# Storing two kinds of attention outputs with ScalarE instead of VectorE in a two-block transformer kernel

## Chip, core and metric

The kernel runs on one core of a Trainium2 chip. The time is that of one execution on the device, in microseconds. TensorE multiplies matrices from SBUF into PSUM (eight banks, `bank0` to `bank7`), VectorE and ScalarE read PSUM and work beside it, GpSimd prepares weights, and SyncE issues the DMAs that load them.

## What is computed

A sequence of 512 tokens of width 1024 goes through two blocks of two layers each. The first block (dilated attention, a gated recurrence, convolutional feed-forward layers) isn't touched. The second block has in each layer three attentions, whose outputs are gated and merged:

```python
o_a = _nsa(nsa_q, nsa_kv, nsa_gate, ...)          # compressed + selected + window attention, 8 heads of 64
o_a = o_a * jax.nn.silu(nsa_silu)
o_b = _fox(fox_qkv, fox_f, ...) * jax.nn.silu(fox_silu)     # forget-gated attention, 8 heads of 64
o_m = _memory_xattn(mem_q, mem_kv, ...) * jax.nn.silu(mem_silu)   # 256 memory keys, 4 heads of 128
u = g[:, :, 0] * (o_a @ w_branch_a[l]) + g[:, :, 1] * (o_b @ w_branch_b[l]) + g[:, :, 2] * (o_m @ w_branch_m[l])
x = x + u @ w_out[l]
```

Each attention is a masked softmax of scaled logits, times the values. Forget-gated and memory attention have the plain form: the value product divided by the sum of the exponentials.

## The kernel before, in words

**Tasks.** The attention of one layer of block two is cut into 128 tasks. A task is one head (a pair for compressed attention) and one tile of 128 queries. They come in four chunks of 32 (`n` = 0 to 3). In a chunk the tiles 0 and 3 are paired, then 1 and 2: two compressed tasks, eight selected and window tasks, four forget-gated (`fox`) and two memory (`mem`) ones. So fox and mem are the tasks 10 to 15 and 26 to 31 of each chunk, 32 and 16 a layer. A task has 128, 256, 384 or 512 keys.

**The pipeline.** Each engine runs through the same steps `now` = 0 to 139, in an order written out by hand, and waits on semaphores. In step `now`:

- TensorE (`pe_attend`): the logits of task `now` (L1920 mem, L1925 to L1927 fox, L1932 to L1934 selected and window, L1917 and L1918 compressed) into bank `now % 3`; then the value product of task `now - 4` (`pe_output`, L1959) into bank 5 or 6; then the transposition of the probabilities of task `now - 2` (L1944) into bank 3 or 4. In some steps a projection of 24 matmuls for a gate follows (L400 to L402, about 5.5 us; three in a chunk, at its steps 11, 18 and 25, in the first chunk at 1, 13 and 23).
- ScalarE (`act_attend`): copies the transposed probabilities of `now - 2` to SBUF (L1972), then makes the exponential of `now` (L1983, followed by a read of the accumulator, which holds the sum). Some steps add a tanh (L2019), copies of queries (L1443, L2009) or of gated outputs (L1997).
- VectorE (`dve_attend`): stores the output of `now - 5` (`dve_store`: L2130 selected and window, L2134 compressed, L2136 fox and mem), the row maximum of the logits of `now` (L2054), the reciprocal of the sum of `now - 1` (L2062), the scaled maximum of `now` (L2068) on which the exponential waits, and further small factors; in some steps halves of gates (L2098, L2104), the gating (L2111), low parts (L1451, L2116) and forget terms (L1815).

**What the stores hold up.** There are two output banks. The value product of a task waits until the store of the task two before has emptied its bank (`c.free[u] = c.s.stored[t.t]`, read by `pe_free`). The row maximum of a task waits for the store of the task six before, since they share a row of `at_st`. At steps 5, 7 and 9 of the next chunk TensorE turns the stored rows back (`pe_back`), and those wait for the last store of their kind. From step 128 on TensorE runs merge projections between the last value products.

Of the kernel before, what the change touches and what calls it, by code (L numbers as in the profile page):

```python
# [10 lines left out]
ACT = mybir.ActivationFunctionType  # L11
ALU = mybir.AluOpType
# [17 lines left out]
HD = 64  # L30
# [39 lines left out]
class Signals:  # L70
    def __init__(self, nc, ctx):
        self.every = []

        def new(name):
            self.every.append(Signal(ctx.enter_context(nc.semaphore(name))))
            return self.every[-1]


        self.unit_loaded = [new(f"unit_loaded_{s}") for s in range(SLOTS)]
        self.gains_loaded, self.ident_loaded = new("gains_loaded"), new("ident_loaded")  # L80
        self.x_loaded = [new(f"x_loaded_{k}") for k in range(DC // 2)]
        self.lru_loaded, self.taps_loaded = new("lru_cols_loaded"), new("taps_loaded")
        self.bias_loaded = [new(f"bias_loaded_{s}") for s in range(2)]
        self.consts_loaded = new("consts_loaded")
        self.w1_loaded, self.mem_loaded = new("cmp_w1_loaded"), new("mem_loaded")
        self.out_stored = new("out_stored")
        self.halves_moved = new("halves_moved")
        self.piece_hi, self.piece_split = new("piece_hi_by_act"), new("piece_split_by_vector")

        self.unit_hi, self.unit_split, self.post_added = new("unit_hi_done"), new("unit_split"), new("post_added")  # L90

        self.unit_multiplied = new("unit_multiplied")
        self.tokens_summed, self.factor_spread = new("tokens_summed"), new("factor_spread")
        self.logits_ready, self.turned = new("logits_ready"), new("turned")
        self.weighted, self.rows_turned = new("values_weighted"), new("rows_turned")
        self.rotated, self.compressed = new("rotated"), new("compressed")

        self.hi_done, self.squared = new("hi_done"), new("squared")
        self.wide_ready, self.bank_copied = new("factor_wide_ready"), new("bank_copied")
        self.exponentials, self.turned_out = new("exponentials_done"), new("turned_copied_out")  # L100
        self.rows_out, self.act_step = new("rows_copied_out"), new("function_applied")
        self.forget_biased = new("forget_biased")

        self.ones_set = new("ones_set")
        self.lo_done, self.factor_found = new("lo_done"), new("factor_found")
        self.evicted, self.residual_added = new("bank_evicted"), new("residual_added")
        self.squares_added, self.dve_step = new("squares_added"), new("vector_step_done")
        self.biased, self.maximum, self.normalized = new("logits_biased"), new("maximum_found"), new("rows_normalized")
        self.stored, self.roped = new("output_stored"), new("roped")
        self.prepared, self.gate_rows, self.short_turned_out = new("layer_prepared"), new("gate_rows_ready"), new("short_turned_copied_out")  # L110
        self.gated = new("output_gated")
        self.widened = new("factor_widened")
# [1734 lines left out]
CHUNK, TASKS, STAGE, LAST_NSA = 32, 128, 5, 25  # L1847
# [51 lines left out]

def pe_back(pe, c, layer, n, j, b):  # L1900

    pe.wait_ge(*c.s.stored["rows", layer, n, j])
    pe_free(pe, c, b)
    for i in range(TT):
        m = pe.matmul(c.bank[b][:, i * P:i * P + P], c.o_rows[n % 2][j][:, i, :], c.ident[:, :], is_transpose=True)
    c.s.rows_turned.on(m, ("back", layer, n, j))
    c.free[b] = c.s.gated["back", layer, n, j]
# [41 lines left out]
def pe_output(pe, c, t):  # L1949
    u = 5 + t.index % 2  # L1950
    o, pt, values = c.bank[u][:, 0:t.width], c.at_pt[t.index % 3], values_of(c, t)
    if t.index == 0:
        pe.wait_ge(*c.s.bank_copied["cmp", t.layer])
    if t.kind == "fox":
        pe.wait_ge(*c.s.rows_out[t.layer, 31 + t.n])
    pe.wait_ge(*c.s.turned_out[t.t])
    pe_free(pe, c, u)
    for s, v in enumerate(values):
        m = pe.matmul(o, pt[:, s * P:s * P + P], v, start=s == 0, stop=s == len(values) - 1)  # L1959
    c.s.weighted.on(m, t.t)  # L1960
    c.free[u] = c.s.stored[t.t]


def act_attend(act, c, layer):
    tasks = tasks_of(layer)
    for now in range(STEPS):
        if 0 <= now - 2 < TASKS:
            t = tasks[now - 2]
            act.wait_ge(*c.s.turned[t.t])
            if t.index >= 3:  # L1970
                act.wait_ge(*c.s.weighted[t.t - 3])
            c.s.turned_out.on(act.activation(c.at_pt[t.index % 3][:, 0:t.keys], c.bank[3 + t.index % 2][:, 0:t.keys], ACT.Copy), t.t)  # L1972
        if now < TASKS:
            t = tasks[now]
            st = c.at_st[t.index % 6]
            act.wait_ge(*c.s.maximum[t.t])
            if t.index >= 3:
                act.wait_ge(*c.s.turned[t.t - 3])
            if t.index < 2:
                act.wait_ge(*c.s.prepared["cmp_blank"])  # L1980
            for h in range(t.heads):
                keys = slice(NCP * h, NCP * h + NC) if t.kind == "cmp" else slice(0, t.keys)
                m = act.activation(probabilities(c, t)[:, keys], c.bank[t.index % 3][:, keys], ACT.Exp,  # L1983
                                   scale=exp_scale(c, t, h), bias=st[:, 2 + h:3 + h], accum_out=st[:, 4 + h:5 + h])
            c.s.exponentials.on(m, t.t)
        n, step = divmod(now, CHUNK)
        if n < 3 and step == LAST_NSA + 1:
            act.wait_ge(*c.s.logits_ready[tasks[now - 1].t])
            act_query_hi(act, c, layer, n + 1)
        if n < 4 and step == STAGE:  # L1990
            act_stage(act, c, layer, n, tasks)
        if n < 4 and step in SILU_ACT[n]:
            act_silu(act, c, layer, n, SILU_ACT[n][step])
        if n and step in BACK_HI:
            j = BACK_HI[step]
            act.wait_ge(*c.s.gated["back", layer, n - 1, j])
            c.s.hi_done.on(act.activation(c.o_hi[j][:, n - 1, :], c.o_all[:, n - 1 + 4 * j, :], ACT.Copy), ("back", layer, n - 1, j))  # L1997
# [39 lines left out]
def dve_attend(dve, c, layer):  # L2037
    z, step, tasks = c.layer_norm(layer), c.s.dve_step, tasks_of(layer)
# [2 lines left out]
    dve.memset(c.fq[0][HD:P, :], 0.0)  # L2041
    c.s.prepared.on(dve.memset(c.fq[1][0:HD, :], 0.0), ("fox_blank", layer))
    for now in range(STEPS):
        if 0 <= now - 5 < TASKS:
            dve_store(dve, c, tasks[now - 5])
        if now < TASKS:
            t = tasks[now]
            st = c.at_st[t.index % 6]
            dve.wait_ge(*c.s.logits_ready[t.t])
            if t.t >= 6:  # L2050
                dve.wait_ge(*c.s.stored[t.t - 6])
            bank = c.bank[t.index % 3]
            logits = bank[:, 0:2 * NCP].rearrange("p (g n) -> p g n", n=NCP)[:, :, 0:NC] if t.kind == "cmp" else bank[:, 0:t.keys]
            dmax = step.on(dve.reduce_max(st[:, 0:t.heads], logits, AX_X))  # L2054
        if 0 <= now - 1 < TASKS:
# [3 lines left out]
            if a.kind == "cmp":  # L2059
                d = step.on(dve.tensor_scalar(sa[:, 6:8], sa[:, 4:6], 0.5, None, ALU.max))  # L2060
# [19 lines left out]
        n, r = divmod(now, CHUNK)  # L2080
# [35 lines left out]
    c.s.lo_done.on(dve.tensor_tensor(c.o_lo[:, n + 4 * j, :], c.o_all[:, n + 4 * j, :], c.o_hi[j][:, n, :].bitcast(F32), ALU.subtract), ("back", layer, n, j))  # L2116


def dve_store(dve, c, t):
    st, o = c.at_st[t.index % 6], c.bank[5 + t.index % 2][:, 0:t.width]  # L2120
    kind = {"fox": 1, "mem": 2}.get(t.kind, 0)
    out = c.o_rows[t.n % 2][kind][:, t.i, t.j * HD:t.j * HD + t.width]
    factor = st[:, 8:9] if t.which is None else st[:, 10:11]
    dve.wait_ge(*c.s.weighted[t.t])
    dve.wait_ge(*c.s.dve_step["factor", t.t])
    if t.n >= 2 and t.kind in ("cmp", "fox", "mem"):
        dve.wait_ge(*c.s.rows_turned["back", t.layer, t.n - 2, kind])
    if t.kind in ("sel", "win"):
        dve.wait_ge(*c.s.stored[t.t - 2])
        m = dve.scalar_tensor_tensor(out, o, factor, out, ALU.mult, ALU.add)  # L2130
    elif t.kind == "cmp":
        def heads(ap):
            return ap.rearrange("p (g d) -> p g d", d=HD)
        m = dve.tensor_tensor(heads(out), heads(o), st[:, 10:12].unsqueeze(2).to_broadcast([P, 2, HD]), ALU.mult)  # L2134
    else:
        m = dve.tensor_scalar(out, o, factor, None, ALU.mult)  # L2136
    d = c.s.stored.on(m, t.t)
    c.s.stored.value["rows", t.layer, t.n, kind] = d[1]

# [401 lines left out]
```

## Time and profile before

| what | value |
| --- | --- |
| time, median of 3 runs | 3016.96 us (3015.71 to 3018.23) |
| the profiled execution, as timed | 3021.99 us |
| its span | 3020.5 us |
| TensorE busy | 2976.1 us (99%) |
| VectorE busy | 1497.1 us (50%) |
| ScalarE busy | 807.1 us (27%) |
| GpSimd busy | 1939.0 us (64%) |

Busy shares are means over the whole program; the two attention stages are 1818 to 2079 us and 2531 to 2792 us. Ends of matmuls are modelled in the profile, so that matmuls overlap in it and short stalls of TensorE show only in part as idle time. Where a stall matters, the start of one instruction is set against the end of the one that it waited for.

### The profile page before, as it was taken

What the parts mean: (1) busy time and instruction counts of PE and PEld (TensorE: products, weight loads), DVE (VectorE), ACT (ScalarE), POOL (GpSimd) and SP (SyncE); (2) the same over time, 40 slices, a digit from 0 to 9 for tenths busy, and PEclk for the clock granted to TensorE, in tenths of its full rate; (3) what the DMA queues carried; (4) which work ended last, traced back from release to release, by engine and by line L of the source; (5) the groups of instructions that cost most, each with busy time, mean ns of one, the idle gap of its engine ahead of it and who ended that gap; (6) DMA issues with size and microseconds to landing.
All of it is one profiled execution on the core that took longest, in us unless ns stands there. A gap on an engine that the chain in (4) does not pass through costs nothing.

```text
span 3020.5 us, 41671 instructions
## 1 busy us (share of the span) xinstructions
PE 2976.1 (99%) x15422; PEld 2495.9 (83%) x15422; DVE 1497.1 (50%) x3021; ACT 807.1 (27%) x1755; POOL 1939.0 (64%) x2192
## 2 busy tenths in 40 slices
PE   9999999999999999999999999999999999999999
PEld 7888887888888878888888887788888988888887
DVE  3333334477730684777213746663334654664332
ACT  1111111322210452222112225552112213564110
POOL 6555554599987788999775862125777684112775
PEclk9999999999999999999999999999999999999999
DMA  4222232122332222323323221011224332011232
GB/s 168 93 90 89 93 105 67 57 98 98 98 98 98 72 82 77 98 98 98 111 91 126 94 95 43 29 36 64 98 98 140 100 103 70 29 43 36 91 98 91
DMA packets 70216, 261.47 MB, mean 87 GB/s; under 512 B 8320, under 2 KB 8832, under 8 KB 68224
## 3 DMA queue, kind: packets, MB, share of 16 engines
q1 hardware_dynamic: 65696, 232.81, 23.6%
q10 hardware_dynamic: 4320, 25.99, 2.4%
q8 instruction: 125, 2.05, 0.3%
q14 instruction: 75, 0.61, 0.1%
HBM read 251.43 MB, written 2.10 MB: 84 GB/s over the span
## 4 chain that ended last, share of the span: by engine, by line
PE 88%; POOL 5%; DVE 3%; issue 2%; ACT 2%; DMA 0%; ACTq 0%; DVEq 0%; SPq 0%; POOLq 0%
PE bank L400 23%; PE bank L402 23%; PE bank L401 23%; POOL w_lo L2314 3%; PE bank L1959 3%; PE bank L1944 1%; PE bank L708 1%; POOL w_hi L2310 1%; PE bank L427 1%; PE bank L440 1%; PE bank L432 1%; PE bank L1660 1%; PE bank L428 1%; PE bank L680 1%; PE bank L1366 1%
## 5 line engine op out<-in xcount | busy, mean ns | idle before, releaser
L2314 POOL TENSOR_TENSOR w_lo<-w_raw,w_hi 128x256 fp32r<-128x256 f32 x1728 | 1406.7, 844 | 36.1
L2310 POOL TENSOR_SCALAR w_hi<-w_raw 128x1024 fp32r<-128x1024 f32 x432 | 489.9, 1134 | 1014.6 <-PE bank L402 918.7
L400 PE MATMUL bank<-in_hi,w_hi 128*128 128x512 f32 x1408 | 554.8, 394 | 0.7 <-POOL w_lo L2314 0.7
L402 PE MATMUL bank<-in_hi,w_lo 128*128 128x512 f32 x1408 | 548.6, 390 | 0.0
L401 PE MATMUL bank<-in_lo,w_hi 128*128 128x512 f32 x1408 | 547.8, 389 | 0.0
L400 PE MATMUL bank<-z_hi,w_hi 128*128 128x512 f32 x976 | 392.4, 402 | 0.4 <-POOL w_lo L2314 0.4
L402 PE MATMUL bank<-z_hi,w_lo 128*128 128x512 f32 x976 | 381.2, 391 | 0.0
L401 PE MATMUL bank<-z_lo,w_hi 128*128 128x512 f32 x976 | 380.7, 390 | 0.0
L402 PEld LDWEIGHTS bank<-in_hi,w_lo 128*128 128x128 f32 x1408 | 264.3, 188 | 56.0
L400 PEld LDWEIGHTS bank<-in_hi,w_hi 128*128 128x128 f32 x1408 | 264.5, 188 | 53.0 <-issue 1.1
L401 PEld LDWEIGHTS bank<-in_lo,w_hi 128*128 128x128 f32 x1408 | 264.7, 188 | 52.8
L400 PEld LDWEIGHTS bank<-z_hi,w_hi 128*128 128x128 f32 x976 | 183.9, 188 | 39.3 <-issue 3.7
L401 PEld LDWEIGHTS bank<-z_lo,w_hi 128*128 128x128 f32 x976 | 184.0, 189 | 38.8 <-issue 2.9
L402 PEld LDWEIGHTS bank<-z_hi,w_lo 128*128 128x128 f32 x976 | 183.5, 188 | 39.3
L2054 DVE TENSOR_REDUCE at_st<-bank 128x1 f32<-128x256 f32 (+4 forms) x256 | 113.0, 441 | 131.9 <-PE bank L1927 69.7
L400 PE MATMUL bank<-ffn_hidden_hi,w_hi 128*128 128x512 f32 x384 | 149.6, 390 | 0.0
L402 PE MATMUL bank<-ffn_hidden_hi,w_lo 128*128 128x512 f32 x384 | 149.4, 389 | 0.0
L401 PE MATMUL bank<-ffn_hidden_lo,w_hi 128*128 128x512 f32 x384 | 149.4, 389 | 0.0
L1972 ACT ACTIVATE at_pt<-bank 128x256 f32<-128x256 f32 (+3 forms) x256 | 104.2, 407 | 163.4 <-PE bank L1944 161.7
L662 DVE TENSOR_TENSOR out_squares<-out_squares,square 128x512 f32<-128x512 f32 x28 | 28.2, 1009 | 229.9 <-ACT square L653 229.7
L1018 DVE TENSOR_TENSOR ffn_raw<-bank,factor_wide 128x512 f32<-128x512 f32 x96 | 65.4, 684 | 116.4 <-PE bank L402 107.8
L772 ACT ACTIVATE logit<-logit,stat 128x768 f32<-128x768 f32 x32 | 30.0, 937 | 281.1 <-DVE stat L830 281.1
(441 smaller groups left out, 5161.5 us busy)
## 6 DMA issues: line engine op xcount, KB each, us to landing
w_raw<-in_units SPq DMA_DIRECT2D x434, 512.0 KB, 3.4
bias<-in_bias ACTq DMA_DIRECT2D x8, 1152.0 KB, 5.1
o_all<-in_cmp_w ACTq DMA_DIRECT2D x4, 2048.0 KB, 8.5
x_res<-in_x ACTq DMA_DIRECT2D x4, 512.0 KB, 7.6
mem_in<-in_mem ACTq DMA_DIRECT2D x2, 1024.0 KB, 8.6
nsa_q_hi<-nsa_q_hi SPq DMA_DIRECT2D x16, 128.0 KB, 2.5
nsa_q_lo<-nsa_q_lo SPq DMA_DIRECT2D x16, 128.0 KB, 2.3
out<-x_res ACTq DMA_DIRECT2D x4, 512.0 KB, 2.6
```

Of the source, the lines that this page charges most:

```text
L400: pe.matmul(out, hi[:, w], rh, start=start and n == 0, stop=False)
L401: pe.matmul(out, hi[:, w], rl, start=False, stop=False)
L402: last = pe.matmul(out, lo[:, w], rh, start=False, stop=stop and n == len(tiles) - 1)
L427: pe.matmul(out, c.w_hi[(first + u) % SLOTS][:, w], hi[:, k, :], start=k == 0, stop=False)
L428: pe.matmul(out, c.w_lo[(first + u) % SLOTS][:, w], hi[:, k, :], start=False, stop=False)
L432: last = pe.matmul(out, c.w_hi[(first + u) % SLOTS][:, w], lo[:, k, :], start=False, stop=k == DC - 1)
L1018: c.s.evicted.on(dve.tensor_tensor(c.raw[half][:, :], c.bank[2 * (n % 3) + half][:, :], z.wide, ALU.mult), ("up", layer, n, half))
L1959: m = pe.matmul(o, pt[:, s * P:s * P + P], v, start=s == 0, stop=s == len(values) - 1)
L1972: c.s.turned_out.on(act.activation(c.at_pt[t.index % 3][:, 0:t.keys], c.bank[3 + t.index % 2][:, 0:t.keys], ACT.Copy), t.t)
L2054: dmax = step.on(dve.reduce_max(st[:, 0:t.heads], logits, AX_X))
L2310: d = c.s.unit_hi.on(pool.tensor_scalar(c.w_hi[s][:, :], c.w_raw[s][:, :], 1.0, 0.0, ALU.mult, ALU.add))
L2314: last = pool.tensor_tensor(c.w_lo[s][:, w], c.w_raw[s][:, w], c.w_hi[s][:, w].bitcast(F32), ALU.subtract)
```

## The change

Fox and mem tasks, 48 a layer, are stored by ScalarE (`act_store`) with one copy that has a scale per partition (the reciprocal). It stands in ScalarE's step `now = t + 4`, behind the exponential, where VectorE stored in its step `t + 5`, at its start. These stores count on a semaphore of their own (`copied_out`), and TensorE's value product, `pe_back` and VectorE's row maximum wait on the one or the other after the kind of task. The new instruction waits for the value product, the factor and, from the third chunk on, for the turning of the rows that it overwrites. Stores of compressed, selected and window tasks stay with VectorE.

```diff
@@ pe_back
-    pe.wait_ge(*c.s.stored["rows", layer, n, j])
+    pe.wait_ge(*(c.s.copied_out if j else c.s.stored)["rows", layer, n, j])
@@ pe_output
-    c.free[u] = c.s.stored[t.t]
+    c.free[u] = stored(c, t)
@@ act_attend, behind the exponential
+        if 0 <= now - 4 < TASKS and by_act(tasks[now - 4]):
+            act_store(act, c, tasks[now - 4])
@@ dve_attend
-        if 0 <= now - 5 < TASKS:
+        if 0 <= now - 5 < TASKS and not by_act(tasks[now - 5]):
             dve_store(dve, c, tasks[now - 5])
...
-                dve.wait_ge(*c.s.stored[t.t - 6])
+                dve.wait_ge(*stored(c, t, 6))
@@ new
+def by_act(t):
+
+    return t.which is None
+
+
+def stored(c, t, back=0):
+    every = tasks_of(t.layer) if t.index >= back else tasks_of(t.layer - 1)
+    t = every[(t.index - back) % TASKS]
+    return (c.s.copied_out if by_act(t) else c.s.stored)[t.t]
+
+
+def act_store(act, c, t):
+    st, o = c.at_st[t.index % 6], c.bank[5 + t.index % 2][:, 0:t.width]
+    kind = {"fox": 1, "mem": 2}[t.kind]
+    act.wait_ge(*c.s.weighted[t.t])
+    act.wait_ge(*c.s.dve_step["factor", t.t])
+    if t.n >= 2:
+        act.wait_ge(*c.s.rows_turned["back", t.layer, t.n - 2, kind])
+    d = c.s.copied_out.on(act.activation(c.o_rows[t.n % 2][kind][:, t.i, t.j * HD:t.j * HD + t.width], o, ACT.Copy, scale=st[:, 8:9]), t.t)
+    c.s.copied_out.value["rows", t.layer, t.n, kind] = d[1]
@@ dve_store
-    else:
-        m = dve.tensor_scalar(out, o, factor, None, ALU.mult)
```

## Rows read from the trace of the kernel before

**Rows 1.** The page: busy us (share of the span) xinstructions of each engine.

```profile
PE 2976.1 (99%) x15422; PEld 2495.9 (83%) x15422; DVE 1497.1 (50%) x3021; ACT 807.1 (27%) x1755; POOL 1939.0 (64%) x2192
```

**Rows 2.** Windows view: length, busy us (instructions) of PE, PEld, DVE, ACT, POOL, then clock, DMA.

```profile
1880.00:1910.00 30.00, 28.12 (x198) 23.83 (x197) 20.75 (x91) 19.42 (x61) 3.82 (x5) 1.00 0.06 19
```

**Rows 3.** The chain that ended last: start us, us, what.

```profile
1904.58 0.53 ACT fox_q L2019
...
1905.73 0.29 DVE o_rows L2136
```

**Rows 4.** Waits in the first attention stage: us in total, times, longest.

```profile
PE bank L1959 <- DVE o_rows L2130: 4.0, 7, 1.0
...
PE bank L1959 <- DVE o_rows L2134: 2.4, 6, 0.5
PE bank L1959 <- DVE o_rows L2136: 1.9, 7, 0.4
```

**Rows 5.** Groups of the whole run by shape, VectorE: busy us, mean ns | idle before.

```profile
L2136 DVE TENSOR_SCALAR o_rows<-bank,at_st 128x64 f32<-128x64 f32 x64 | 17.8, 278 | 10.5 <-PE bank L1959 10.5
...
L2136 DVE TENSOR_SCALAR o_rows<-bank,at_st 128x128 f32<-128x128 f32 x32 | 11.1, 347 | 22.9 <-PE bank L1959 22.9
```

**Rows 6.** The same of ScalarE.

```profile
L1972 ACT ACTIVATE at_pt<-bank 128x512 f32<-128x512 f32 x48 | 28.5, 594 | 21.7 <-PE bank L1944 21.6
...
L1983 ACT ACTIVATE cmp_p<-bank,at_st,nsa_scale 128x31 f32<-128x31 f32 x64 | 23.6, 373 | 3.4 <-DVE at_st L2066 2.9
...
L1972 ACT ACTIVATE at_pt<-bank 128x128 f32<-128x128 f32 x80 | 21.9, 274 | 75.7 <-PE bank L1944 75.5
...
L1983 ACT ACTIVATE at_p<-bank,at_st,nsa_scale 128x128 f32<-128x128 f32 x32 | 14.7, 458 | 9.6 <-DVE at_st L2068 9.4
...
L1469 ACT ACTIVATE fox_q<-bank,both_layers_cols 128x512 f32<-128x512 f32 x8 | 5.5, 687 | 42.5 <-PE bank L402 42.5
```

**Rows 7.** Instructions in order of time: start us, us, engine, line [idle before].

```profile
1833.33 0.19 ACT L1983 ACTIVATION_READ_ACCUMULATOR at_p<-bank,at_st,nsa_scale 128x1 f32 x1
...
1833.58 0.33 PE L1944 MATMUL bank<-ident,at_p 128*128 128x128 f32 x1
...
1833.66 0.48 PE L1932 MATMUL bank<-win_k_parts,nsa_q_hi 128*128 128x512 f32 x1
```

**Rows 8.** The same: stretch A, second chunk of the first stage.

```profile
1905.59 0.22 ACT L1983 ACTIVATION_READ_ACCUMULATOR at_p<-bank,at_st,mem_scale 128x1 f32 x1
...
1905.73 0.28 DVE L2136 TENSOR_SCALAR o_rows<-bank,at_st 128x64 f32<-128x64 f32 x1
...
1905.93 0.42 DVE L2054 TENSOR_REDUCE at_st<-bank 128x1 f32<-128x256 f32 x1
...
1906.16 0.41 PE L1959 MATMUL bank<-fox_v,at_pt 128*128 128x64 f32 x2 [0.26 <-DVE o_rows L2136]
...
1906.63 0.56 ACT L1983 ACTIVATE at_p<-bank,at_st,mem_scale 128x256 f32<-128x256 f32 x1 [0.29 <-DVE at_st L2068]
...
1906.93 1.08 PE L1959 MATMUL bank<-fox_v,at_pt 128*128 128x64 f32 x8
1907.09 0.19 ACT L1983 ACTIVATION_READ_ACCUMULATOR at_p<-bank,at_st,mem_scale 128x1 f32 x1
```

**Rows 9.** The same: stretch B.

```profile
1916.51 0.34 DVE L2136 TENSOR_SCALAR o_rows<-bank,at_st 128x128 f32<-128x128 f32 x1
...
1919.28 0.28 DVE L2134 TENSOR_TENSOR o_rows<-bank,at_st 128x128 f32<-128x128 f32 x1
...
1919.71 0.52 PE L1959 MATMUL bank<-sel_v,at_pt 128*128 128x64 f32 x3 [0.52 <-DVE o_rows L2134]
```

**Rows 10.** The same: stretch C.

```profile
1938.86 0.20 ACT L1983 ACTIVATION_READ_ACCUMULATOR at_p<-bank,at_st,mem_scale 128x1 f32 x1
...
1938.92 0.86 PE L1959 MATMUL bank<-fox_v,at_pt 128*128 128x64 f32 x6
...
1946.78 0.41 PE L1959 MATMUL bank<-sel_v,at_pt 128*128 128x64 f32 x2 [0.28 <-DVE o_rows L2134]
```

More of the change, by code:

```diff
@@ L87, in __init__ @@
         self.halves_moved = new("halves_moved")
+        self.copied_out = new("output_copied_out")
         self.piece_hi, self.piece_split = new("piece_hi_by_act"), new("piece_split_by_vector")
@@ L2116, in dve_back_lo @@
     c.s.lo_done.on(dve.tensor_tensor(c.o_lo[:, n + 4 * j, :], c.o_all[:, n + 4 * j, :], c.o_hi[j][:, n, :].bitcast(F32), ALU.subtract), ("back", layer, n, j))
+def by_act(t):
[13 more added lines that the diff above has]
+    c.s.copied_out.value["rows", t.layer, t.n, kind] = d[1]
 def dve_store(dve, c, t):
     st, o = c.at_st[t.index % 6], c.bank[5 + t.index % 2][:, 0:t.width]
-    kind = {"fox": 1, "mem": 2}.get(t.kind, 0)
+    kind = 0
     out = c.o_rows[t.n % 2][kind][:, t.i, t.j * HD:t.j * HD + t.width]
-    factor = st[:, 8:9] if t.which is None else st[:, 10:11]
+    factor = st[:, 10:11]
     dve.wait_ge(*c.s.weighted[t.t])
     dve.wait_ge(*c.s.dve_step["factor", t.t])
-    if t.n >= 2 and t.kind in ("cmp", "fox", "mem"):
+    if t.n >= 2 and t.kind == "cmp":
         dve.wait_ge(*c.s.rows_turned["back", t.layer, t.n - 2, kind])
@@ L2130, in dve_store @@
         m = dve.scalar_tensor_tensor(out, o, factor, out, ALU.mult, ALU.add)
-    elif t.kind == "cmp":
+    else:
         def heads(ap):
```

## Prediction

> **What bounds the kernel now.** I read first the busy time by engine: TensorE is busy for 99% of the span [rows 1]. Only what makes TensorE wait can move the time. The change lies in the two attention stages (1818 to 2079 us and 2531 to 2792 us), so I cut one of them into stretches of 30 us. In such a stretch TensorE has 28.1 us of work, VectorE 20.8, ScalarE 19.4 [rows 2]. Neither helper is full, and both stand idle for some 5 us under each gate projection (12 a stage), so their sums say little. What counts is the order between projections, where TensorE, ScalarE and VectorE hand the tasks round. The chain that ended last shows it: it leaves TensorE, goes through ScalarE's tanh and VectorE's queue to a store of an output, and from that store back to TensorE's next value product [rows 3]. The wait view puts a number on it for the first stage: TensorE's value products stood waiting for a store 20 times, 8.3 us in all (4.0 + 2.4 + 1.9), of which the stores that move (L2136) ended 7 times and 1.9 us [rows 4]. Recorded idle understates it, since matmul ends are modelled, but the order of sizes is plain: two stages, 3.8 us, are what these stores cost TensorE directly.
>
> **What is removed.** 96 stores leave VectorE: 64 of 278 ns and 32 of 347 ns [rows 5], 28.9 us. In a full queue one takes less: the row maximum behind the store at 1905.73 starts 0.20 us after it [rows 8], and behind a memory store, with the same overlap of 0.08, some 0.26 us after it. Two waits of VectorE go with them.
>
> **What is added: the price of one store on ScalarE.** The trace before has no scaled copy of 64 columns by ScalarE. A plain PSUM copy takes 274 ns for 128 columns and 594 for 512, so 0.83 ns a column; a scale per partition makes the 512-column copy 687 instead of 594, so 93 ns more [rows 6]. That gives 274 - 53 + 93 = 0.31 us for 64 columns and 0.37 for 128. From above it is bounded by the exponentials, which have a scale and a bias per partition: 373 ns for 31 columns, 458 for 128, so 0.40 and 0.45. From below by the plain copy carried to 64 columns, 0.22 (0.27 for 128). I take 0.31 and 0.37, since that row has the same function and the same kind of scale. In a full queue ScalarE's instructions follow 0.10 us before the recorded end, so a store delays the next ScalarE work by 0.21 or 0.27 us. All its other operands are old: the factor is from three steps earlier, the rows that it overwrites were turned a chunk and more before, and the value product stands in TensorE's queue ahead of the transposition for which ScalarE's copy in that step waited already. So the new waits cost ScalarE nothing that I can find. No DMA and no queue of SP or GpSimd is passed.
>
> **The hand-over.** The value product of task t+2 waits for the bank of task t. From a VectorE store it starts 0.14 us after the end (1905.73 + 0.28, then 1906.16). From ScalarE the nearest case is the logits of a task that wait for the exponential in their bank: 1833.33 + 0.19, then 1833.66, again 0.14 [rows 7]. The transposition behind the same exponential started at 1833.58, after 0.06; I keep 0.05 as the lower end. I take 0.14, since logits and value product both wait for a bank, the transposition for its input.
>
> **The walk, stretch by stretch.** The store moves from the start of VectorE's step t+5 to the end of ScalarE's step t+4. That sounds earlier, but it stands behind the exponential of task t+4, and the product of t+2, which needs the bank, precedes in TensorE's queue the transposition of t+4. So far that product ran while the exponential ran; now it comes after exponential and store. With the starts of the trace:
>
> Stretch A, tasks 42 to 50 in the second chunk, from its first projection to its second. Exponential 46 ends at 1905.81 [rows 8]. The store of 42 then runs 1905.71 to 1906.02 instead of 1905.73 to 1906.01 on VectorE, and the product of 44 starts at 1906.16 as before: nothing won, though this is the very stall of rows 3. VectorE's maximum of 47 comes 0.20 earlier (1905.73), so exponential 47 starts at 1906.43 instead of 1906.63 and ends at 1907.08 instead of 1907.28. The store of 43 ends at 1907.29 and the product of 45 starts at 1907.42, where it started at 1906.93: 0.49 late. The later ones are covered by that, and TensorE enters the projection 0.49 us late. The projection is TensorE's own work, so nothing is made up in it.
>
> Stretch B, to the third projection. VectorE's memory store at 1916.51 stood between its projection's half-gate and the maximum of task 52; without it exponential 52, the tanh, the gate and the store at 1919.28 come 0.26 earlier, and the product at 1919.71, which waited for that store, too [rows 9]: -0.26.
>
> Stretch C, tasks 58 to 75. Exponential 63 ends at 1939.06; its store of 59 ends 1939.27, so the product at 1938.92 starts at 1939.41, 0.49 late [rows 10]. With 62 the lateness reaches 0.58. Then VectorE, rid of three stores (0.2 + 0.26 + 0.26) in a part where it was last, brings exponential 67 0.25 earlier, and at 1946.78, where the product waits for a compressed-task store that stays on VectorE, only 0.06 is left.
>
> A stage has A three times (+1.47), B three times (-0.78), C twice and once into the merge (+0.06, +0.04, +0.24), and the first chunk, whose projections lie otherwise: +0.60 and +0.06 by the same walk. Sum +1.7 us a stage, **+3.4 us** for two. At both upper ends of price and hand-over it is +6.2, with the lower ends of both -0.9. The profiled execution (span 3020.5 us, 3022.0 as timed) would come to 3025.4; it lies 0.17% above the median of the runs, 3016.96. From that: **3020.4 us**, 0.11% more. In the last steps the stores stand under merge projections of TensorE, on either engine, and cost nothing; if that cover were gone, three hand-overs of about 0.5 us would show.
>
> **The Trainium skill beside it.** VectorE is busy for 20.8 of 30 us, 69% [rows 2], so it isn't full. The Trainium skill, Perfetto Trace Analysis, "Optimizing Scalar/DVE Operations", holds that giving work to ScalarE may make sense if VectorE is saturated; by that rule this move has nothing to win. By the cycle table of the Trainium skill, VectorE: DVE Perf Modes, "The TRN2 errata", a PSUM read of 64 columns costs 197 ns on ScalarE and 192 on VectorE; an estimate by that page is +0.5 us in sum. Its figures for the plain copies, 250 and 570 ns, lie under the 274 and 594 of the rows, and no run here shows a store at 197 [rows 6].
>
> **Rivals.** (1) Slower beyond 0.2%: the store costs ScalarE as much as an exponential of its size, 0.40 and 0.45. Place: the end of ScalarE's steps in stretches A and C, ahead of the next copy and the product. Between the walks at 0.31 and 0.40 the sum rises from 3.4 to 6.2, some 3.2 us for each 0.1 us of price, so from 0.39 on it passes 6 us: +6.2 to 3023.2 at 0.40, +7.8 to 3024.8 at 0.45. For it speaks that the waits may keep the 0.10 us overlap from ScalarE; against it the 93 ns of rows 6. (2) It evens out: price near 0.22 to 0.28, hand-over 0.05 to 0.14; -0.9 to +2, so 3016 to 3019, no change to be seen. For it: ScalarE waits for VectorE's scaled maximum often, and the store fits there. (3) The relief is real: the 3.8 us of direct waits go and B's 0.26 comes six times (1.6) while A costs nothing; -5.4, 3011.6. Against it: in A the exponential itself ends when the old store did. (4) The change does not touch what TensorE waits for at all, because compressed and selected tasks' stores end most of the waits (13 of 20, 6.4 of 8.3 us in rows 4): 0, 3017.
>
> **Chances.** Forecast (+2 to +6): 0.52. Rival 2: 0.18. Rival 4: 0.10. Rival 1: 0.14. Rival 3: 0.06. About 0.2% (6.0 us) is what a measurement can tell from no change: slower by more 0.15 (rival 1 and the forecast's edge), faster by more 0.04, within 0.81. The range takes in -0.9 less some 1.5 of scatter between runs (3015.7 to 3018.2 in three), and rival 1 up to 0.45: 3014.5 to 3025.0.
>
> **What would show it.** L2136 gone from VectorE and 96 scaled copies of about 0.31 and 0.37 us on ScalarE, each right behind an accumulator read. TensorE's waits for VectorE's stores fall from 20 a stage, and waits of L1959 for ScalarE's new store appear at tasks 45 and 61. Within the second chunk, its second projection starts 0.5 us later after its first than now, and its third 0.26 us sooner after the second. A price above 0.39 or a copy that waits behind the store makes it wrong upwards; ScalarE idle before the stores makes it wrong downwards.

## The result

The median of the changed kernel over 20 runs is 3025.57 us, that of the kernel before, over 20 runs, 3021.91 us. The ratio is 1.0015, with a 95% interval of 1.0009 to 1.0020: slower, but by less than the 0.2% that counted as no change. (This ratio and those below weigh all runs and are not the quotients of the two medians.) One of the 20 runs took 7270 us at a full clock and is left out of the ratio and of everything below; without it the median is 3025.49. The two profiled executions say the same, 3025.65 us (span 3024.2, granted clock 0.997) against 3021.99 (span 3020.5, 0.997): +3.7 us. The prediction was +3.4 us and 3020.4 us. So the difference was met within 0.3 us and the absolute time was not: 3025.57 lies 0.6 us above the range's upper end of 3025.0.

The page of the changed kernel, as in [rows 1]:

```profile
PE 2977.1 (98%) x15414; PEld 2496.6 (83%) x15422; DVE 1479.6 (49%) x2925; ACT 826.1 (27%) x1851; POOL 1941.0 (64%) x2192
```

96 instructions have gone over: VectorE has 2925 instead of 3021 and 17.5 us less work, ScalarE 1851 instead of 1755 and 19.0 us more. (VectorE's 96 stores were 28.9 us by their own durations; time in which two of its instructions overlap counts once in the busy time.) TensorE is as full as before.

The new stores in the groups of ScalarE by shape (busy us, mean ns | idle before), with the copies and exponentials that answer to [rows 6] (in the changed kernel matmul, copy and exponential lines are 1 higher than before, VectorE's row maxima, factors and gates and ScalarE's tanh 3; VectorE's stores are L2155 for L2130 and L2159 for L2134, GpSimd's split is L2337 for L2314):

```profile
L1973 ACT ACTIVATE at_pt<-bank 128x512 f32<-128x512 f32 x48 | 28.7, 598 | 24.0 <-PE bank L1945 24.0
...
L1984 ACT ACTIVATE cmp_p<-bank,at_st,nsa_scale 128x31 f32<-128x31 f32 x64 | 23.8, 386 | 2.9 <-DVE at_st L2069 2.9
...
L2140 ACT ACTIVATE o_rows<-bank,at_st 128x64 f32<-128x64 f32 x64 | 20.5, 321 | 0.0
...
L2140 ACT ACTIVATE o_rows<-bank,at_st 128x128 f32<-128x128 f32 x32 | 11.5, 359 | 21.8 <-PE bank L1960 21.8
```

They cost 0.32 and 0.36 us. The 64 of the forget-gated tasks never found ScalarE idle ahead of them (0.0): each stands in a full queue.

The waits in the first attention stage, as in [rows 4] (us in total, times, longest):

```profile
DVE at_st L2065 <- ACT at_p L1984: 17.7, 36, 1.1
...
ACT at_p L1984 <- DVE at_st L2071: 9.0, 16, 1.4
...
PE bank L1960 <- ACT o_rows L2140: 4.8, 14, 0.7
...
PE bank L1960 <- DVE o_rows L2155: 4.1, 7, 1.0
...
PE bank L1960 <- DVE o_rows L2159: 1.0, 3, 0.3
```

The value products' waits for a store were 20, of 8.3 us in all; now they are 24, of 9.9 us. The second stage has the same counts. VectorE's stores end 10 of them instead of 20, but where its plain stores ended 7 (1.9 us), ScalarE's end 14 (4.8 us).

Stretch A in order of time, where [rows 8] stand for the kernel before:

```profile
1900.10 0.58 ACT L1984 ACTIVATE at_p<-bank,at_st,mem_scale 128x256 f32<-128x256 f32 x1
...
1900.55 0.22 ACT L1984 ACTIVATION_READ_ACCUMULATOR at_p<-bank,at_st,mem_scale 128x1 f32 x1
1900.64 0.33 ACT L2140 ACTIVATE o_rows<-bank,at_st 128x64 f32<-128x64 f32 x1
...
1900.84 0.62 ACT L1973 ACTIVATE at_pt<-bank 128x512 f32<-128x512 f32 x1
...
1901.12 0.41 PE L1960 MATMUL bank<-fox_v,at_pt 128*128 128x64 f32 x2 [0.26 <-ACT o_rows L2140]
...
1901.39 0.56 ACT L1984 ACTIVATE at_p<-bank,at_st,mem_scale 128x256 f32<-128x256 f32 x1
...
1901.95 0.30 ACT L2140 ACTIVATE o_rows<-bank,at_st 128x64 f32<-128x64 f32 x1
```

```profile
1902.40 0.85 PE L1960 MATMUL bank<-fox_v,at_pt 128*128 128x64 f32 x6 [0.45 <-ACT o_rows L2140]
```

The store of task 42 ends at 1900.97, and the product of 44 starts 0.15 later. Counted from the start of the chunk's first projection, that is 11.74 us; it was 11.76, so nothing is won. The next one is the damage. The exponential behind it comes 0.22 earlier against that projection than it did (12.01 instead of 12.23), but the store of 43 ends only at 1902.25, and the product of 45 starts at 1902.40 having waited for it, 13.02 us behind the projection instead of 12.53. That is the 0.49.

What it does to the whole stretch is to be read from the first matmul of each gate projection. Four of them, from the second chunk's first to the third chunk's first, in the kernel before:

```profile
1894.40 0.47 PE L400 MATMUL bank<-z_hi,w_hi 128*128 128x512 f32 x1
...
1908.91 0.48 PE L400 MATMUL bank<-z_hi,w_hi 128*128 128x512 f32 x1
...
1923.05 0.48 PE L400 MATMUL bank<-z_hi,w_hi 128*128 128x512 f32 x1
...
1955.70 0.47 PE L400 MATMUL bank<-z_hi,w_hi 128*128 128x512 f32 x1
```

and in the changed kernel:

```profile
1889.38 0.47 PE L401 MATMUL bank<-z_hi,w_hi 128*128 128x512 f32 x1
...
1904.38 0.47 PE L401 MATMUL bank<-z_hi,w_hi 128*128 128x512 f32 x1
...
1918.45 0.48 PE L401 MATMUL bank<-z_hi,w_hi 128*128 128x512 f32 x1
...
1951.16 0.47 PE L401 MATMUL bank<-z_hi,w_hi 128*128 128x512 f32 x1
```

The gaps were 14.51, 14.14 and 32.65 us and are 15.00, 14.07 and 32.71: A +0.49, B -0.07, C +0.06. Such starts are free of the modelled ends and of what lies ahead of the stage. Followed to the last merge projection, the first stage is 2.14 us longer and the second 2.20. **The stages' sum, +4.34 us,** is the measure for all experiments below.

### The profile page after: what moved, and what is told of

Same layout as the page of the kernel before. It is cut to its first block, busy times and chain, and to the rows that moved or that the text cites. A ratio compares the mean times of both kernels' runs of the same rounds, so it can differ in the third digit from the quotient of the medians.

```text
span 3024.2 us, 41663 instructions
## 1 busy us (share of the span) xinstructions
PE 2977.1 (98%) x15414; PEld 2496.6 (83%) x15422; DVE 1479.6 (49%) x2925; ACT 826.1 (27%) x1851; POOL 1941.0 (64%) x2192
## 4 chain that ended last, share of the span: by engine, by line
PE 88%; POOL 5%; DVE 2%; issue 2%; ACT 2%; DMA 0%; ACTq 0%; DVEq 0%; SPq 0%; POOLq 0%
PE bank L401 23%; PE bank L403 23%; PE bank L402 23%; PE bank L1960 3%; POOL w_lo L2337 3%; PE bank L1945 1%; PE bank L709 1%; POOL w_hi L2333 1%; PE bank L428 1%; PE bank L433 1%; PE bank L441 1%; PE bank L429 1%; PE bank L1661 1%; PE bank L681 1%; ACT at_p L1984 1%
## 5 line engine op out<-in xcount | busy, mean ns | idle before, releaser
L2337 POOL TENSOR_TENSOR w_lo<-w_raw,w_hi 128x256 fp32r<-128x256 f32 x1728 | 1408.2, 846 | 36.0
```

Source lines behind the costliest of these rows:

```text
L2337: last = pool.tensor_tensor(c.w_lo[s][:, w], c.w_raw[s][:, w], c.w_hi[s][:, w].bitcast(F32), ALU.subtract)
```

## The experiments

Each kernel is the changed one with one further edit, unless it says otherwise. "Sum" is how much longer both attention stages are than in the kernel before, from the projections' starts in one trace each. Within a trace the same gap agrees from chunk to chunk to about 0.1 us; the one stray is a gap of the memory-only kernel, +0.34 in its first stage and 0.00 in its second.

### The store ahead of the copy

```diff
@@ act_attend
+        if 0 <= now - 4 < TASKS and by_act(tasks[now - 4]):
+            act_store(act, c, tasks[now - 4])
         (copy of the transposed probabilities of now - 2, exponential of now)
-        if 0 <= now - 4 < TASKS and by_act(tasks[now - 4]):
-            act_store(act, c, tasks[now - 4])
```

> The changed kernel with ScalarE's store moved to the head of its step, ahead of the copy of the transposed probabilities, so that it no longer stands behind the exponential of the same step. All else is as changed. Order theory (the loss comes from the value product waiting behind exponential and store): the loss of 0.5 us before the second projection of a chunk goes, and VectorE's relief is left; walked with the measured price (0.32 and 0.36 us) and hand-over (0.14 us) each stage is 2.5 us shorter than before, less up to 0.5 us where the relief meets GpSimd: sum -4 to -5 us against before. Load theory (ScalarE has no room for 19 us of busy time more, wherever it stands): +3 to +4 us, as the changed kernel.

Sum -3.55 us (-1.65 and -1.90). The store costs the same or more:

```profile
L2140 ACT ACTIVATE o_rows<-bank,at_st 128x64 f32<-128x64 f32 x64 | 21.2, 331 | 20.5 <-PE bank L1960 20.4
...
L2140 ACT ACTIVATE o_rows<-bank,at_st 128x128 f32<-128x128 f32 x32 | 12.5, 392 | 50.9 <-PE bank L1960 50.9
```

The 20.5 us of idle time ahead of the forget-gated ones are not room in the steps that decide: they are four waits of some 5 us while TensorE runs a projection, and two of 0.2. The other 58 of the 64 stand in as full a queue as before. What has changed is the wait for them. Among the waits of the first stage those of the value product for ScalarE's store are gone, and VectorE's are left:

```profile
PE bank L1960 <- DVE o_rows L2155: 4.0, 7, 1.0
...
PE bank L1960 <- DVE o_rows L2159: 2.9, 6, 0.7
```

ScalarE does 0.01 and 0.03 us more per store, and the kernel gains 7.9 us over the changed one. So it is the order and not the load. The sum that was expected, -4 to -5, was missed by 0.45 us at the least: its upper end already had the gate products that meet GpSimd (836 to 843 ns here; their experiment comes below) in it, and with those gone, under "Both", the sum is -4.48 where the walk had -5. No run shows what the rest is. The timed median (12 runs) was 3019.2 us against 3018.17, ratio 0.9998 (0.9987 to 1.0008), which can't tell it from the kernel before; the section on the prediction says why the median hides 3.5 us.

### The store between copy and exponential

```diff
@@ act_attend
         (copy of the transposed probabilities of now - 2)
+        if 0 <= now - 4 < TASKS and by_act(tasks[now - 4]):
+            act_store(act, c, tasks[now - 4])
         (exponential of now)
-        if 0 <= now - 4 < TASKS and by_act(tasks[now - 4]):
-            act_store(act, c, tasks[now - 4])
```

> The changed kernel with ScalarE's store between the copy of the transposed probabilities and the exponential. Order theory: the store no longer stands behind the exponential, but delays it where ScalarE is the last: walked -2.8 us in the two stages against before, -1.9 with the gate products that meet GpSimd, between the changed kernel and the one with the store at the head. Load theory: +3 to +4 us, as wherever it stands.

Sum -1.51 us (-0.72 and -0.79), with stores of 338 and 399 ns, the dearest of all. The three places give +4.34 (last), -1.51 (middle), -3.55 (first) for the same work: the earlier in the step, the better. It should have been -2.8, or -1.9 with the contention shown further below: the sign was right, the gain overrated by 0.4 us, which no run here explains; the store delays the exponential behind it by 0.2 us, and the dearer store would fit, but neither was tried apart. One timed run, 3022.96 us at 0.996.

### One kind of task alone

```diff
 def by_act(t):
-    return t.which is None
+    return t.kind == "fox"
@@ dve_store: the branch for memory tasks is back
```

> Only the forget-gated tasks are stored by ScalarE, behind the exponential; the memory tasks go back to VectorE. Order theory: all of the loss before each second projection stays (it comes from tasks 43 and 59, both forget-gated), and the relief before each third projection (from a memory store off VectorE) is gone: +4.2 us against before, no shortening between second and third projection. Load theory: 20.5 of the 32.0 us that ScalarE spends on stores, so 64% of the changed kernel's +4.3 us: +2.8 us.

Sum +4.26 us (+2.22 and +2.04); median 3027.26 us, ratio 1.0024 (1.0015 to 1.0033). And the other way round, `t.kind == "mem"`:

> Only the memory tasks are stored by ScalarE, behind the exponential; the forget-gated tasks go back to VectorE. Order theory: no loss before the second projections of chunks 1 to 3, some 0.3 us once before the third of chunk 0, relief of 0.08 to 0.26 us before each third projection: -0.7 us against before, up to +0.2 if the relief meets GpSimd as in the changed kernel. Load theory: 11.5 of 32.0 us, 36% of +4.3: +1.5 us.

Sum +0.22 us (+0.33 and -0.11); median 3017.84 us, ratio 1.0001 (0.9992 to 1.0010). That is the expectation's case in which the relief meets GpSimd, and the gate products do take 829 to 832 ns here. The two sums add up to 4.48 against 4.34 for both kinds together, so they hardly touch one another, and the loss is all in the forget-gated stores, which come four in a row. The memory stores, two in a row behind them, come out even.

### GpSimd's split held back

In stretch B the prediction had -0.26 and the trace shows -0.07 to -0.15. What ran there, in the kernel before:

```profile
1916.60 2.10 POOL L2314 TENSOR_TENSOR w_lo<-w_raw,w_hi 128x256 fp32r<-128x256 f32 x3
...
1918.02 0.62 ACT L2019 ACTIVATE fox_q<-o_all 128x512 f32<-128x512 f32 x1
1918.67 0.69 DVE L2104 SCALAR_TENSOR_TENSOR o_all<-fox_q,o_all 128x512 f32<-128x512 f32 x1
```

and in the changed kernel:

```profile
1912.09 2.11 POOL L2337 TENSOR_TENSOR w_lo<-w_raw,w_hi 128x256 fp32r<-128x256 f32 x3
...
1913.26 0.62 ACT L2022 ACTIVATE fox_q<-o_all 128x512 f32<-128x512 f32 x1
1913.91 0.84 DVE L2107 SCALAR_TENSOR_TENSOR o_all<-fox_q,o_all 128x512 f32<-128x512 f32 x1
```

The relief did arrive: against GpSimd's work, which follows the projection, the tanh and VectorE's gate product come some 0.26 earlier. But GpSimd's subtraction used to end 0.03 us into the product, and now it ends 0.29 us into it (1914.20), and the product takes 0.84 instead of 0.69. That is so at all six places (829 to 837 ns, 692 to 694 before) and at none of the other 18; the subtraction itself takes 0.73 us in both kernels. To tell it from a coincidence, the last quarter of that split was made to wait for the product:

```diff
@@ the split of weights on GpSimd
+    held = {("silu", layer, 3 * n + 1): (layer, n, 1) for layer in range(2) for n in (1, 2, 3)}
...
+            if quarter == 3 and c.order[u - SLOTS] in held:
+                pool.wait_ge(*c.s.dve_step["silu", *held[c.order[u - SLOTS]]])
```

> The changed kernel, with GpSimd's last quarter of one weight split held back until VectorE's gate product in step 21 of chunks 1 to 3 is done (six places). Contention theory (the gate product took 0.84 us instead of 0.69 because it now runs beside that quarter, and so ate the relief): the six products are back at 0.69 us, the stretch between second and third projection is 0.23 us shorter than before instead of 0.08 to 0.11, and the sum is 0.9 us less than the changed kernel's, +3.4 us against before. If the longer product has another cause: it stays at 0.84 us, and the sum at +4.3.

Sum +3.47 us (+1.74 and +1.73). All the gate products of this kernel, as one line's instructions (duration in ns min/median/max, first and last start):

```profile
L2107 DVE SCALAR_TENSOR_TENSOR o_all<-fox_q,o_all x24: 679/692/693, 1829.2 to 2772.7; 128x512 f32<-128x512 f32 x24
```

B is now -0.22 to -0.29. Median 3025.14 us, ratio 1.0016 (1.0007 to 1.0024).

### Both

The store first in the step, and the split held.

```diff
@@ act_attend: as in the store ahead of the copy
@@ the split of weights on GpSimd: as above
```

> ScalarE's store at the head of its step, and GpSimd's last quarter held back in the six places. Order and contention theories together: the two attention stages are 3.6 us shorter than before by the store at the head alone, and the six gate products give back another 0.1 to 0.15 us each: -4.2 to -4.5 us in the two stages; the time of the whole follows by so much less what the granted clock does in between (ratio 0.9985 if that evens out). Load theory: no gain against before.

Sum -4.48 us (-2.24 twice); median 3012.42 us of 11 runs against 3018.11, ratio 0.9988 (0.9979 to 0.9997). It is the fastest of all, and the interval of its ratio leaves out 1. The two medians lie 5.7 us apart because seven of its 11 runs had a mean granted clock of 0.999 and six of the 15 of before; among those runs alone it is 3012.0 against 3015.9, 3.9 us less, which is closer to the 4.48 of the stages. Its first matmuls of the same four projections:

```profile
1894.35 0.47 PE L401 MATMUL bank<-z_hi,w_hi 128*128 128x512 f32 x1
...
1908.71 0.48 PE L401 MATMUL bank<-z_hi,w_hi 128*128 128x512 f32 x1
...
1922.61 0.48 PE L401 MATMUL bank<-z_hi,w_hi 128*128 128x512 f32 x1
...
1954.90 0.47 PE L401 MATMUL bank<-z_hi,w_hi 128*128 128x512 f32 x1
```

Gaps of 14.36, 13.90 and 32.29: A -0.15, B -0.24, C -0.36. Within A:

```profile
1904.91 0.31 ACT L2140 ACTIVATE o_rows<-bank,at_st 128x64 f32<-128x64 f32 x1
...
1905.67 0.41 PE L1960 MATMUL bank<-fox_v,at_pt 128*128 128x64 f32 x2
...
1905.81 0.34 ACT L2140 ACTIVATE o_rows<-bank,at_st 128x64 f32<-128x64 f32 x1
...
1906.73 1.07 PE L1960 MATMUL bank<-fox_v,at_pt 128*128 128x64 f32 x8
```

These are the stores of tasks 42 and 43 and the products of 44 and 45 that need their banks. The stores end 0.45 and 0.58 us ahead of them, where it was 0.14 for both, and in stretch C 0.4 to 0.9 for all six. The store is no longer what the product waits for.

### The price of a store

The slope, "some 3.2 us for each 0.1 us", came from the walk alone. A copy of one column ahead of each store makes it dearer:

```diff
@@ act_store
+    act.activation(st[:, 6:7], st[:, 8:9], ACT.Copy)
     d = c.s.copied_out.on(act.activation(...))
```

> The changed kernel with one more ScalarE copy of a single column, without use, ahead of each store; it makes the store dearer by what such a copy takes in the queue. By the walk the two stages lose 3 to 5 us for each 0.1 us: for 0.12 us more +7.6, for 0.16 +9.6, for 0.20 +11.7 us against before. If ScalarE had idle time in these steps to hide the store, the loss would stay near +4.3.

```profile
L2141 ACT ACTIVATE o_rows<-bank,at_st 128x64 f32<-128x64 f32 x64 | 21.0, 327 | 0.0
L2140 ACT ACTIVATE at_st<-at_st 128x1 f32<-128x1 f32 x96 | 20.0, 208 | 21.4 <-PE bank L1960 21.4
```

Sum +7.46 us (+3.66 and +3.80), 3.12 more than without it; one timed run, 3023.66 us at 0.999, where the changed kernel had 3020.9. The copy is recorded with 208 ns, but the store starts only 0.09 behind it, so the step is some 0.09 longer: 3.5 us for 0.1. The opposite is a store without its factor. This kernel leaves out the division by the sum of the exponentials for forget-gated and memory tasks:

```diff
-    d = ...(act.activation(c.o_rows[...], o, ACT.Copy, scale=st[:, 8:9]), t.t)
+    d = ...(act.activation(c.o_rows[...], o, ACT.Copy), t.t)
```

> The changed kernel with stores on ScalarE that have no scale, so the division by the sum of the exponentials is left out for forget-gated and memory tasks. The store should take 0.22 to 0.23 us for 64 columns and 0.27 for 128, 93 ns less; by the walk the two stages then lose +1.2 us against before, with the six longer gate products +2.1. If the loss came from the waits and not from the price it would stay at +4.3.

```profile
L2140 ACT ACTIVATE o_rows<-bank 128x64 f32<-128x64 f32 x64 | 14.2, 222 | 0.0
L2140 ACT ACTIVATE o_rows<-bank 128x128 f32<-128x128 f32 x32 | 8.5, 267 | 22.1 <-PE bank L1960 22.1
```

Sum +1.89 us (+0.95 and +0.94); one timed run, 3017.55 us at 0.999. The factor costs 99 ns with 64 columns and 92 with 128, and 2.45 us of the sum, 2.5 for 0.1. So even a store as cheap as a plain copy loses when it stands last in the step.

## Why the prediction was right in its difference and wrong in its time

**The price: right.** 0.31 and 0.37 us were put together from a plain copy, 0.83 ns a column and 93 ns for a scale [rows 6]; measured were 0.321 and 0.359 us, and without the scale 0.222 and 0.267, where the lower bounds were 0.22 and 0.27. The next copy starts 0.20 to 0.25 us after a store starts; the prediction had 0.21 and 0.27. The Trainium skill, ScalarE: Activation LUTs, "What ACT_TABLE_LOAD costs", gives 186 ns and 0.833 ns a column for an activation with constants, and some 93 more for each operand with a value per partition; by it the stores would have been an estimated 332 and 386 ns, and the difference with and without factor agrees with the runs (99 and 92). The cycle table that the prediction cited from the Trainium skill, VectorE: DVE Perf Modes, "The TRN2 errata", with 197 ns for 64 columns, missed by 25 ns even where there is no factor, and by 124 with it.

**The hand-over: right.** 0.14 us from the end of ScalarE's store to the value product, as from the exponential in [rows 7]; the trace has 0.14 at tasks 42, 43, 47 and at all of 58 to 63.

**Stretch A and C: right.** A was +0.49 by the walk and +0.49 to +0.51 by the trace, three times a stage. C was +0.06 and +0.04 and +0.24 into the merge, and came as +0.05 or 0.06, +0.02 or 0.03 and +0.24; the waits at tasks 45 and 61 are there. The first chunk was +0.66 and came as +0.57 and +0.66.

**Stretch B: right in its mechanism, the term too large.** The forecast was -0.26 six times, measured -0.07 to -0.15 (-0.6 in sum instead of -1.56). The working let the relief run through exponential, tanh, gate and store at their old durations. It said that no queue of GpSimd is passed and didn't ask what runs beside the gate product once it starts 0.26 earlier: the last quarter of GpSimd's subtraction, which lengthens it by 0.15. With the subtraction held back, B was the -0.26 that was forecast, within 0.04. These 0.9 us are the difference between the +3.4 of the walk and the measured 4.34, and the kernel with the split held, +3.47, is the walk's kernel. That the medians differ by 3.66 us and so come closer to +3.4 than the stages do is luck: the median of a batch goes with its mix of the clock, as shown next.

**The base: wrong, and this is the step that put the time outside the range.** "It lies 0.17% above the median of the runs, 3016.96. From that: 3020.4 us", with "some 1.5 of scatter between runs (3015.7 to 3018.2 in three)". The median of three was taken as the kernel's time with 1.5 us of scatter around it, and the profiled execution, at 3022.0, was set aside as an odd one. Measured were a base of 3021.91 over the 20 runs set beside the changed kernel, 5 us higher, and single runs from 3015.7 to 3024.1. The other runs of the same kernel, with their mean granted clock, show that it was not odd:

| mean granted clock of the run | before: runs, median us | changed: runs, median us | difference |
| --- | --- | --- | --- |
| 0.999 | 10, 3016.4 | 5, 3020.9 | +4.5 |
| 0.998 | 9, 3018.1 | 3, 3024.5 | +6.4 |
| 0.997 | 13, 3022.1 | 8, 3026.2 | +4.1 |

(Before: the 33 runs beside the first experiments, of which one more was at 0.995; changed: the 20 runs, of which three more were at 0.996, median 3027.7.) The kernel has steps of time, some 6 us from 0.999 to 0.997, and each batch of runs mixes them as it comes: the median of before was 3016.96 in the three, 3021.91 with 17 more beside them, and 3018.17 and 3018.11 in two other batches of 33 and 15. With the profiled execution as base, the prediction's own 3025.4 would have been 0.2 us from the median that was measured. That closeness is luck as well: a batch of before with a median of 3018.1, as the two later ones had, and the stages' 4.34 would by estimate have given 3022.5, inside the range. What was wrong is the choice of one step for the base and a scatter of 1.5 us where the steps span 6; which side of 3025.0 a batch then falls on is chance. The three runs gave no hint of the upper step; the fourth, the profiled one, did. At equal clock the difference is +4.1 to +4.5 in the two larger rows, which is the 4.34 of the stages, and at 0.998 the changed kernel has three runs only.

Where the steps come from can be seen in windows of the two profiled executions (length, busy us of PE, PEld, DVE, ACT, POOL, then clock, DMA). The kernel before:

```profile
1613.00:1626.00 13.00, 13.00 (x81) 11.47 (x79) 8.92 (x11) 1.68 (x4) 10.34 (x11) 1.00 0.25 83
1626.00:1639.00 13.00, 13.00 (x58) 12.52 (x57) 1.19 (x3) 3.02 (x8) 1.25 (x2) 0.50 0.26 64
```

and the changed kernel:

```profile
2367.00:2379.00 12.00, 12.00 (x80) 10.83 (x78) 9.18 (x22) 1.18 (x2) 9.36 (x10) 0.99 0.21 78
2379.00:2389.00 10.00, 10.00 (x45) 9.71 (x45) 3.66 (x21) 1.57 (x5) 0.36 (x1) 0.50 0.17 52
```

The granted clock falls from 2.4 to 1.2 GHz for 13.65 us at 1626 in the one and for 10.2 us at 2379 in the other, though TensorE was busy for all of the 12 or 13 us ahead of it. The ten traces of this case have falls of this kind, 3.4 to 13.65 us long, at about 1626 (three traces), 2340 (three) and 2375 (three), and none of them in three traces; TensorE was busy for all of the 12 us ahead of each. A shorter one at about 1115, behind 5 us in which TensorE was busy for 0.2 to 3.1, stands in all ten, and most have one in the last 3 us. What one costs can be read between the stages, from the first matmul of the merge behind the first stage's gates (2097.56 in the kernel before) to the first gate projection of the second stage (2531.43): 433.9 us in the four traces without a fall there, 435.5 with one of 3.4 us, 438.8 with 10.2 and 440.3 to 440.8 in the four with 13.65. So a fall of 13.65 us costs 6.4 to 6.9, about one step of the table. From the second stage's merge to the end it is 210.4 us in all ten, with up to 2.6 us of fall at the end or with none: that fall lowers a run's mean clock and costs nothing that shows. So the rows of the table are coarse. What sets the falls off is not shown.

This is why the first stage starts 5.59 us sooner in the changed kernel's trace than in that of before, though the change can't have made it so, and the second one 1.45 later: the starts of a stage tell nothing of the change, the gaps in it do. And it is why the store-first kernel's median of 3019.2 shows no gain: five of its 12 runs were at 0.996, two lower still, and three at 0.998 or above. At equal clock it gains 3.1 to 3.6 us (3015.0 against 3018.1 at 0.998, 3018.5 against 3022.1 at 0.997, two of its runs each; 3013.0 against 3016.4 at 0.999, one run). Whether the changed orders also make such falls more frequent is left open: at 0.996 or less were one of the 48 runs of before whose clock is on record, three of 19 of the changed kernel, and seven of the 12 of this one; in its profiled run, at 0.996, 2.6 us of the falls are those at the end.

**The rivals.** Rival 1, the store at an exponential's price, falls: 0.32 and 0.36 are not 0.40 and 0.45. Its slope of 3.2 us for 0.1 holds, 2.5 downwards and 3.5 upwards. Rival 2 (even) needed a price of 0.22 to 0.28; at 0.222 and 0.267 the sum is +1.9, inside its -0.9 to +2, so it was well formed and its condition wasn't met. Rival 3 (the relief is real, -5.4) falls for this change. But it is near what the change is worth in another place: -3.55 with the store at the head of the step, -4.48 with the split held back as well. So it did not follow from VectorE's 69% in [rows 2] that nothing was to be won. Rival 4 (no effect) falls by the 14 waits for ScalarE's stores and the +4.34.

**What would show it.** L2136 was gone from VectorE, and 88 of the 96 new stores stood behind accumulator reads; the other eight come at the end of a stage, where no exponential is left. The waits for VectorE's stores fell from 20 to 10 a stage. A was 0.49 late. The one that failed was the third projection "0.26 us sooner after the second": it was 0.07 sooner.

## What to carry to other kernels

When an instruction moves to another engine, its price counts less than its place in that engine's step: put it where its operand is ready and where no engine waits for it behind other work, here ahead of the copy (-3.55 us) and not behind the exponential (+4.34). Follow a relief instruction by instruction to where it lands, and ask of each what it now runs beside. And take as the base of a forecast of 0.1% not the median of three runs, but the runs at one granted clock, the profiled one among them.

## What the runs showed of the hardware

A product on VectorE of two float tiles in SBUF (128x512) takes 0.69 us, and 0.84 when a GpSimd subtraction of SBUF tiles that began 0.44 before it runs on 0.29 into it; where the subtraction ends only 0.03 into the product, nothing is lost (six places of each). The Trainium skill, SBUF — State Buffer, "SBUF: two separate sides", says that a VectorE instruction with two SBUF inputs and a GpSimd instruction that reads SBUF share a pair of ports, which the one that starts first keeps until it ends, while the other is blocked. The trace agrees in kind: the one that came second is the longer one, and the first is not (0.73 us either way). It differs in size: if the product had been blocked for the whole overlap it would have taken 0.98 us; it took 0.83 to 0.84, half of the 0.29 more.

A scale of one value per partition costs ScalarE 92 to 99 ns a copy. A one-column copy is recorded with 208 ns but delays the next instruction by only 0.09, as a store of 321 ns delays it by 0.20.
